# A two-block transformer kernel in float32: the compression branch gets a lane of its own with GELU in four steps, and the first loads are issued and split in another order

## What is computed

```
def first_block(x, mix_norm, w_in, b_in, ...):
    xn = rms_norm(h, mix_norm[l])
    proj = jnp.einsum("bsd,dp->bsp", xn, w_in[l]) + b_in[l]
    q, k, v, cb, cc, cx, ga, gc = jnp.split(proj, splits, axis=-1)
...
    def compress(src, w1, w2):
        blocks = src.reshape(B, S, G, dk)[:, blk_idx] + cmp_pos[None, None, :, None, :]
        blocks = blocks.transpose(0, 3, 1, 2, 4).reshape(B, G, n_cmp, CMP_BLOCK * dk)
        return jax.nn.gelu(blocks @ w1) @ w2

    kc = compress(kc_src, w_ck1, w_ck2)
    vc = compress(vc_src, w_cv1, w_cv2)
```

## Time and profile before

| what | value |
|---|---|
| median of three runs | 1093.68 us (1093.56, 1093.68, 1098.21) |
| profiled execution, its own time | 1097.8 us |
| its span | 1095.5 us |
| PE busy | 1063.8 us (97%) |
| DVE, ACT, POOL busy | 621.8, 446.3, 27.5 us |
| mean granted clock of TensorE | 0.993 |
| PE idle at the start, before its first matmul | 8.06 us |

### The profile page before, as it was taken

The page is one execution under the profiler, slowest core; times in us unless marked ns, Lnnn a source line. Parts: engine busy times, 40 slices in busy tenths (PEclk is TensorE's granted clock), DMA queues, the critical chain, the costliest instruction groups (busy, mean ns, idle before and its releaser), DMA issues.

```text
span 1095.5 us, 13942 instructions
## 1 busy us (share of the span) xinstructions
PE 1063.8 (97%) x5454; PEld 848.8 (77%) x5454; DVE 621.8 (57%) x1179; ACT 446.3 (41%) x823; POOL 27.5 (3%) x41
## 2 busy tenths in 40 slices
PE   6999999999999999999999999999999988999997
PEld 5877778888879888888888888988877765666575
DVE  5457654444355666642666634544696863566757
ACT  5344333233254444321444433444345434566640
POOL 0000000000011000000000000200000001000000
PEclk9999999999999999999999999999999988999999
DMA  7421123323331823341223233242112021511011
GB/s 265 154 78 58 58 77 95 98 97 96 118 115 60 312 96 97 111 139 58 82 92 105 92 139 125 93 129 92 58 58 67 24 84 54 196 40 39 20 59 77
DMA packets 29103, 107.06 MB, mean 98 GB/s; under 512 B 3226, under 2 KB 3370, under 8 KB 28400
## 3 DMA queue, kind: packets, MB, share of 16 engines
q1 hardware_dynamic: 24288, 84.04, 23.2%
q0 software_dynamic: 4032, 19.96, 5.3%
q10 hardware_dynamic: 720, 2.20, 0.5%
HBM read 101.44 MB, written 7.36 MB: 99 GB/s over the span
## 4 chain that ended last, share of the span: by engine, by line
PE 88%; issue 5%; DVE 3%; ACT 2%; DMA 1%; POOL 0%; ACTq 0%; DVEq 0%; POOLq 0%; SPq 0%
PE ps L695 26%; PE ps L697 25%; PE ps L696 24%; PE ps L1077 2%; PE ps L1111 2%; PE ps L1094 1%; PE ps L972 1%; PE ps L836 1%; PE ps L809 1%; PE ps L821 1%; PE ps L1044 1%; DMA XT<-xt 1%; PE ps L711 1%; PE ps L961 0%; PE ps L1049 0%
## 5 line engine op out<-in xcount | busy, mean ns | idle before, releaser
L695 PE MATMUL ps<-XH,whi 128*128 128x512 f32 (+1 forms) x864 | 338.6, 392 | 9.6 <-DVE wlo L1534 8.1
L697 PE MATMUL ps<-XH,wlo 128*128 128x512 f32 (+1 forms) x864 | 328.3, 380 | 0.0
L696 PE MATMUL ps<-XL,whi 128*128 128x512 f32 (+1 forms) x864 | 328.0, 380 | 0.0
L1515 DVE TENSOR_TENSOR wlo<-raw,whi 128x1024 fp32r<-128x1024 f32 (+1 forms) x158 | 189.2, 1204 | 154.9 <-ACT whi L1176 154.5
L695 PEld LDWEIGHTS ps<-XH,whi 128*128 128x128 f32 x864 | 163.5, 189 | 50.5 <-issue 18.0
L1176 ACT CAST whi<-raw 128x1024 fp32r<-128x1024 f32 (+1 forms) x158 | 161.2, 1026 | 85.9 <-PE ps L697 57.9
L697 PEld LDWEIGHTS ps<-XH,wlo 128*128 128x128 f32 x864 | 163.4, 189 | 31.5
L696 PEld LDWEIGHTS ps<-XL,whi 128*128 128x128 f32 x864 | 163.8, 190 | 27.5 <-issue 0.2
L695 PE MATMUL ps<-whi,GH 128*128 128x512 f32 x176 | 68.8, 391 | 0.0
L696 PE MATMUL ps<-wlo,GH 128*128 128x512 f32 x176 | 68.5, 389 | 0.0
L697 PE MATMUL ps<-whi,GL 128*128 128x512 f32 x176 | 68.5, 389 | 0.0
(11 more groups left out here) (280 smaller groups left out, 1343.0 us busy)
## 6 DMA issues: line engine op xcount, KB each, us to landing
raw<-wp SPq DMA_DIRECT2D x150, 512.0 KB, 3.5
vec_dram<-row_dram POOLq DMA_DIRECT2D x1, 3072.0 KB, 13.0
H<-x POOLq DMA_DIRECT2D x1, 2048.0 KB, 8.1
x_dram<-H POOLq DMA_DIRECT2D x1, 2048.0 KB, 7.6
A<-w1c POOLq DMA_DIRECT2D x2, 1024.0 KB, 6.8
A<-x_dram POOLq DMA_DIRECT2D x1, 2048.0 KB, 12.2
y<-A SPq DMA_DIRECT2D x8, 256.0 KB, 2.0
raw<-wp SPq DMA_DIRECT2D x4, 402.0 KB, 3.5
```

The lines of the kernel that those rows point to most:

```text
L695: self.e.matmul(o, ah, bh, start=start, stop=False)
L696: self.e.matmul(o, ah, bl, start=False, stop=False)
L697: return self.e.matmul(o, al, bh, start=False, stop=stop)
L1515: self.e.tensor_tensor(wlo[BUF[i]][:, 0:w], raw[i % NR][:, 0:w], whi[BUF[i]][:, 0:w].bitcast(F), ALU.subtract).then_inc(sems["lo"], 1)
```

## The change

**Start.** ACT's queue keeps only `PPt`. SP issues, in this order: first half of slot 0, x piece 0, second half of slot 0, x piece 1; then waits for `wa` (first half landed) and issues piece 2, waits for x0 and issues piece 3, waits for x1 and issues slot 1, waits for x2 and issues slot 2. ACT and DVE split the first half of slot 0 first, then tiles 0 to 2, the second half, tiles 3 to 7, and slot 1 last. PE runs `warm`, ten 128x128 matmuls of ones into bank 7, then all of slot 0, then all of slot 1. Slot 3 goes to bank 6, slot 4 to bank 0; the convolution's ring then starts at bank 1. `v` also waits for `rsc` 4. `q` has four parts rather than two, with `roots` at the same place among PE's matmuls.

**Compression.** It starts at turn 37 with one step a turn, and GELU is four steps: `c_square` (ACT), `c_gelu` (DVE, three operations), `c_exp` (ACT), `c_last` (DVE, three operations). Turns: move(0) 37, blk(0,0) 38, blk(0,1) 39, move(1) 40, mm(0,0..3) 41 to 44, square(0) and blk(1,0) 45, gelu(0) and blk(1,1) 46, exp(0) 47, last(0) 48, mm(1,0..3) 49 to 52, square(1) 53, gelu(1) 54, exp(1) 55, last(1) 56, end 57. The second `c_move` now stands ahead of the load of `W1` in POOL's queue.

```
+ring((1, 2, 0), [(SLOT_CONV + i, 0, "rsc", SCALED_CONV + i + 1) for i in range(12)]
...
+     ring((0, 1, 2, 6), [(SLOT_Q + i, 0, "rsc", i + 1) for i in range(5)]))
...
     def compress():
+        en.c_move(0)
+        yield
         for i in range(2):
-            en.c_move(i)
+            en.c_square(i - 1)
             en.c_blk(i, 0)
             yield
+            en.c_gelu(i - 1)
             en.c_blk(i, 1)
+            yield
+            if i == 0:
+                en.c_move(1)
+            else:
+                en.c_exp(0)
+                yield
+                en.c_last(0)
             yield
             for l in range(4):
                 en.c_mm(i, l)
                 yield
+        en.c_square(1)
+        yield
+        en.c_gelu(1)
+        yield
+        en.c_exp(1)
+        yield
+        en.c_last(1)
         yield
         en.c_end()
         yield
...
-    weave(projections(), (hgrn(), 4, 45 / 54), (stick(), 32, 1), (compress(), 42, 14 / 16))
+    weave(projections(), (hgrn(), 4, 45 / 54), (stick(), 32, 1), (compress(), 37, 1))
...
+            def warm(self):
+                self.wait_ge("ec", 3)
+                for n in range(10):
+                    self.e.matmul(ps[7][:, 0:128], ONE[:, :], ONE[:, :], start=True, stop=True)
...
             def v(self, t):
                 self.wait_ge("rt", 2)
+                self.wait_ge("rsc", 4)
...
                 e.dma_start(PPt[:, :], pp).then_inc(sems["pp"], 16)
-                for n, (k0, k1) in enumerate(XT_PARTS):
-                    e.dma_start(XT[:, k0:k1, :], xt[:, k0:k1, :]).then_inc(sems[f"x{n}"], 16)
...
+            def c_square(self, i):
+                if i >= 0:
                     self.wait_ge("cm", i + 1)
                     self.wait_ge("hc", 3 * i)
                     self.e.activation(GE, ps[6][:, 0:62], ACT.Square).then_inc(sems["gx"], 1)
...
             e.dma_start(raw[0][:, 0:512], wp[0, :, 0:512]).then_inc(sems["wa"], 16)
+            first_x(0)
             e.dma_start(raw[0][:, 512:1024], wp[0, :, 512:1024]).then_inc(sems["w0"], 16)
+            first_x(1)
+            met.wait_ge("wa", 16)
+            first_x(2)
+            met.wait_ge("x0", 16)
+            first_x(3)
             for i in range(1, N_SLOTS):
-                if i == 2:
-                    met.wait_ge("x2", 16)
+                if i < NR:
+                    met.wait_ge(f"x{i}", 16)
```

More of the change, by code:

```diff
@@ L169, in idle @@
         pass
-    begin = first = sums = roots = split = split_all = split_hi = split_lo = norm_rest = turn = part = fm = idle
+    begin = warm = first = sums = roots = split = split_all = split_hi = split_lo = norm_rest = turn = part = fm = idle
     q = k = v = qk = soft = tr = cp = pv = fin = ft = cc = cx = cb = gate = branch = merge = wout = idle
@@ L175 @@
     h_start = h_diag = h_q1 = h_prep = h_mult = h_off = h_prod = h_pick = h_pv = h_norm = idle
-    c_move = c_blk = c_mm = c_end = begin_norm = block2_after = idle
+    c_move = c_blk = c_mm = c_square = c_gelu = c_exp = c_last = c_end = begin_norm = block2_after = idle
     n_qk = n_scale = n_tr = n_pv = n_out = nsa_begin = s_first = s_soft = s_second = s_mask = s_pv = mix_mul = mix_tile = mix_rows = last = out2 = end = idle
@@ L241, in stages @@
     en.begin()
+    en.warm()
     en.first()
@@ L245, in stages @@
     en.split(3)
-    en.q(2, 0)
+    for part in range(2):
+        en.q(2, part)
     en.roots()
-    en.q(0, 1)
-    en.q(1, 1)
+    en.q(2, 2)
+    en.q(0, 3)
+    en.q(1, 3)
     en.split(4)
-    en.q(2, 1)
+    en.q(2, 3)
     slot(SLOT_Q + 3)
-    en.q(3, 0)
-    en.q(3, 1)
+    for part in range(4):
+        en.q(3, part)
     slot(SLOT_K)
@@ L786, in rows, with q @@
                     f.then_inc(sems["tm"], 1)
-            def q(self, i, half):
+            def q(self, i, part):
                 if i > 1:
-                    self.tile(SLOT_Q + i, half, 2, 0)
+                    self.tile(SLOT_Q + i, part, 4, 0)
             def k(self, half):
@@ L1207, in turn, with q @@
                     self.e.copy(XH[:, 4 * c:4 * c + 4, t * P:(t + 1) * P], c4(ps[NORM_BANKS[t][c]][:, :])).then_inc(sems["xh"], 1)
-            def q(self, i, half):
-                if half:
+            def q(self, i, part):
+                if part == 3:
                     q = Q[:, i, :]
@@ L1531, in first @@
             def first(self):
-                self.first_x(0)
                 self.wait_ge("hi", 1)
@@ L1900, in c_blk, with c_gelu @@
                         self.e.tensor_tensor(BLK[r, 8 * a:8 * a + 8, g, :], sv, pos, ALU.add).then_inc(sems["blk"], 1)
-            def c_mm(self, i, part):
-                if part == 3:
+            def c_gelu(self, i):
+                if i >= 0:
                     x = ps[6][:, 0:62]
@@ L2039, in begin, with q @@
                 e.memset(ONE[:, :], 1.0).then_inc(sems["ec"], 1)
-            def q(self, i, half):
-                if i == 2 and half == 0:
+            def q(self, i, part):
+                if i == 2 and part == 0:
                     self.wait_ge("x3", 16)
```

41 lines of the change are left out of this document (21 added, 20 removed).

## The result

| | before | after |
|---|---|---|
| median beside one another, us | 1093.62 (1092.89 to 1098.21, 4 runs) | 1085.51 (1085.15 to 1086.88, 4 runs) |
| profiled execution, us | 1097.8 | 1085.15 |
| its span, us | 1095.5 | 1083.1 |
| mean granted clock | 0.993 | 0.998 |

The ratio after to before is 0.9919, with a 95% interval of 0.9891 to 0.9948: 0.8% faster. The forecast was 1081.8 us, its range 1077.0 to 1087.5. In the experiments one of the ten executions of `bank_only` took 1326.47 us at a mean clock of 0.752 and is left out.

What follows compares the result with a forecast made beforehand. PE was taken to bound the kernel, losing time to waits, mostly for DVE, and half-clock stretches. From 1097.8 us, start -4.05 and second block -10.9 gave 1082.9; leaning on the gap between runs, 1081.8 was forecast, range 1077 to 1087.5.

Steps and rivals of the forecast that it cites:

- loads and pace of the start: Start: reordered loads and warm let PE begin at 6.2 us and roots at 22.15 us, 2.65 us earlier.
- wait at turn 51, clock behind it: Second block: the earlier exchange and c_blk remove PE's 3.65 us wait, and the half-clock stretch behind it, 2.75 us.
- wait at turn 57, clock behind it: Second block: GELU in steps cuts PE's 2.98 us wait to 1.4, and the clock holds, giving back 3.1 us.
- pause at turn 40: c_blk(0,0) ahead of s_soft(0,2) makes PE wait 1.5 us longer, 1.85 in all; the clock holds.
- two small waits: Second block: waits of 0.3 and 1.0 us go because PE's added products fill them, 1.3 us saved.
- lean on the gap between runs: Faster runs of before probably lacked a half-clock stretch, so 1081.8 us was taken rather than 1082.9.
- Rival D: DVE becomes the bound in turns 38 to 48, with pauses and half-clock stretches: 14.7 us more, 1096.5; chance 0.03.
- A: Rival: the pause at turn 57 still drops the clock, so 3.1 us come back: 1085; chance 0.13.
- Rival C: DVE in turns 38 to 40 pauses PE over 1.85 us and drops the clock, +3 us: 1084.8; chance 0.08.
- x1 makes 1.41 MB, 6.1 + 0.3 = 6.4: Start: by the measured transfer curve, the second piece of x lands at 6.4 us, where it came at 8.3 before.
- rival B: Start: chained loads cost what the order gives, pieces 2 and 3 come 2 us later; term 1 -2.2, 1083.7; chance 0.10.
- Rival E: Start: pace stays at 0.43 us a matmul into slot 1; term 1 -1.4 to -3, 1083 to 1084.5; chance 0.07.

Runs made afterwards that it cites:

- bank_only: Kernel before with only the bank changes (slot 3 in bank 6, slot 4 in bank 0, ring from bank 1, v waiting for rsc 4); 1095.39 us, ratio 0.9994.
- Exchange_first: Kernel before with the second exchange issued at turn 44, ahead of the load of W1; 1090.92 us, ratio 0.9944.
- gelu_at_once: Changed kernel with the whole GELU of the second block in one turn (55) rather than in steps; 1089.49 us, ratio 0.9941.
- blk_later: Changed kernel with c_blk(0,0) and c_blk(0,1) one turn later, at turns 39 and 40; 1084.51 us, ratio 0.9897.
- after_again: Changed kernel once more, unedited, in a later batch; 1086.4 us, ratio 0.9898.
- no_warm: Changed kernel without the filler matmuls ahead of slot 0; 1085.24 us, ratio 0.9903.
- x1_ahead: Changed kernel with the second piece of x issued ahead of the second half of slot 0's weights; 1085.45 us, ratio 0.9903.
- start_only: Kernel before with only the start's changes (loads, first, warm, banks), compression as before; 1093.0 us, ratio 0.9962.

## Why the prediction was right, and where it was off

The median fell by 8.1 us, where 11.9 were forecast, and by 12.65 from the profiled run of before to that of after, where 14.9 were.

| step | forecast | measured |
|---|---|---|
| loads and pace of the start | -2.65 | -1.0 (`roots` 25.02 to 24.00) |
| bank of slot 3 | -1.4 | -1.4 to -1.6 |
| wait at turn 51, clock behind it | -3.65, -2.75 | -3.65, gone |
| wait at turn 57, clock behind it | -1.6, -3.1 | -1.7 (2.98 to 1.30), gone |
| pause at turn 40 | +1.5 (1.85) | +1.5 (1.83) |
| two small waits | -1.3 | -0.3: two others came, 0.52 and 0.42 |
| lean on the gap between runs | -1.1 | 0 |

**The second block** was right in its mechanism and close in its sizes, -10.9 against -10.0. Exchange_first shows that the place behind `W1` made 1.7 us of the first wait (the stretch behind it was gone with it in its one profile), gelu_at_once that GELU in steps took 2.6 us off turn 57, blk_later that DVE's order made the wait at turn 40. The 1.4 us forecast for turn 57 came from two small slips that nearly cancel: by the timeline of before PE would be free at 908.94, not 908.75 (909.86 less the 0.92 us of `c_mm`), and DVE's two operations released it 1.53 us after their start rather than 1.45, which gives the measured 1.3. The missing 0.9 are the two waits for L1907 at 871.98 and 875.36: I had said that small waits would go, since PE's added products fill them, and counted DVE's slack for `s_second` alone. `h_prod` waits for the same queue, and found it late in the very turns that I had called near DVE's limit. Rival D did not come: there is no wait for L1992 between turns 41 and 56. Nor did A: nine profiles have the short wait at turn 57, 1.28 to 1.30 us, and all kept the clock. Rival C, a half-clock stretch behind turn 40, was absent in the profiled run but came in after_again and no_warm.

**The start** is the term that was mis-sized. Its step "x1 makes 1.41 MB, 6.1 + 0.3 = 6.4" failed: x1 landed at 7.7 us.

```profile
XT<-xt SPq DMA_DIRECT2D x1, 512.0 KB, 5.6
```

In after the core moved 177 GB/s in the first 5 us and 376 in the next 2.7 (windows), so 1.39 MB by 6.4 us: the curve was right. But by 7.7 us, when x1 landed, it had moved 1.90 MB. The queues of the first 7.7 us (packets, MB, share), and SP's issues of pieces 2 and 3 (timeline), say whose bytes these were:

```profile
q1 hardware_dynamic: 699, 1.80, 69.3%
q10 hardware_dynamic: 144, 0.10, 4.7%
...
3.99 0.33 SPq L2151 DMA_DIRECT2D XT<-xt  x1
...
4.90 0.33 SPq L2151 DMA_DIRECT2D XT<-xt  x1
```

SP's queue (q1) had moved 1.80 MB. All that SP had issued up to x1 is 1.31 MB, and the 0.10 MB on ACT's queue are the parameters, so at least 0.49 MB belonged to pieces 2 and 3, issued at 3.99 and 4.90 us. I had taken the bytes to move in the order of issue, x1's all ahead of piece 2's; the pieces behind moved beside it. This is read from the bytes; no run issues pieces 2 and 3 later, so it is not tested. From there pieces 2 and 3 followed about 1 us late (DVE's five tiles end at 13.9, not 12.8). So the start came out near rival B's -2.2 (-2.4 to -2.6), but chiefly by x1, which waits for no other piece. Rival B's support was misread as well: the earlier trace rows's 2.2 us are not the shortest landing of before, where the eight stores of `y`, 256 KB each, landed in 2.0 us in the median. x1_ahead, the one other order that was tried, did not mend it.

The Trainium skill, *DMA: Bandwidth & Descriptors*, "Issuing engines are not separate DMA queues", says that the DMAs of all engines end up on the same 16 DMA engines and interleave. The trace of before agrees: in its first 5 us SP's queue moved 0.63 MB and ACT's 0.36 MB side by side. The section "Anatomy of one DMA", which the prediction names beside it, is about DMAs issued from POOL (GpSimd); the pieces of the start go by SP's queue.

The second cause is the clock. I let `warm` bring the fast pace near 7 us and keep it; it came at 6.71 in after, for three matmuls, was lost from 9.36 to 12.8, and in after_again it was not there at all until 13.1. Rival E, the slow pace into slot 1, did not come: even in gelu_at_once, where it lasted longest of the five (to 14.75 us), it ended within slot 0. By blk_later, which kept the fast pace and had its piece 0.4 us earlier, the stretch cost at most 0.8 us.

**The gap between profile and median** was read rightly in kind: the start_only run and the clocks of the 15 runs of before show executions with one stretch less. But I took 1.1 us off for it, and after has no such stretch to lose in its profiled run (1085.15 against a median of 1085.51). The three runs shown at first had two of the less common sort, and the four of the result three: in the experiments 5 of 39 runs of before took 1093.8 us or less. That is also why the gain is 8.1 us by one pair of medians and 10.9 by another (1097.29 and 1086.4).

**The rule "1.85 us leaves the clock at 1.00"**, against rivals A and C, rested on one row and doesn't hold (table below). That it held in the profiled run was luck.

## What to carry to other kernels

Look for what stands in a queue in front of a small transfer: 128 KB behind 1 MB came 3.3 us late, and that cost 1.7 us of waiting and, in the profiled runs of that order, a stretch at half clock behind it. Put work that nobody waits for a turn away from the operation that TensorE does wait for, and count DVE's slack for every wait of TensorE in that stretch, not for the longest one. When transfers are laid on a bandwidth curve, count those issued behind the one in question too, up to its landing, and judge an edit of 1 or 2 us by landmarks in the trace, since the time scatters by more.
